# A PEER expert stage in two parts: U rows and dots first, then half of V's columns dense on TensorE and half gathered for VectorE

## What is computed

```python
q  = normalize((h @ wq).reshape(t, 8, 256))           # 8 heads
s1 = einsum('thd,hkd->thk', q[..., :128], subkeys[:, 0])   # 128 keys per half
s2 = einsum('thd,hkd->thk', q[..., 128:], subkeys[:, 1])
# top 16 of each half, top 16 of the 16 x 16 sums: 16 experts per token and head
idx  = i1 * 128 + i2                                   # of 16384 experts
gate = softmax(best_scores)
act  = gelu(einsum('td,tkd->tk', h, peer_u[idx]))      # 128 dots per token
out  = einsum('tk,tkd->td', act * gate, peer_v[idx])   # 128 rows added per token
y    = layer_norm(alpha * h_in + gt2 * out)
```

## Time and profile before

| | |
|---|---|
| median of three runs | 3455.93 us |
| span of the profiled execution | 3455.3 us (its time is not given apart from the span) |
| TensorE busy | 3200.0 us, 93% |
| VectorE busy | 1851.0 us, 54% |
| GpSimd busy | 918.8 us, 27% |
| ScalarE busy | 525.4 us, 15% |
| DMA moved | 989.40 MB, mean 286 GB/s; 420 to 428 GB/s from 2200 us to 3400 us |
| gathers | 536.90 MB, 37.0% of what 16 DMA engines could be busy |

### The profile page before, as it was taken

One profiled execution on the slowest core, in us unless ns is written; L12 is line 12 of the kernel. 1 busy time (PEld: TensorE's weight loads), 2 busy tenths in 40 slices (PEclk: granted clock), 3 DMA queues, 4 the chain that ended last, 5 costly groups with the idle time before them and its releaser, 6 DMA issues. The chain is left out here.

```text
span 3455.3 us, 30801 instructions
## 1 busy us (share of the span) xinstructions
PE 3200.0 (93%) x10108; PEld 1775.5 (51%) x10108; DVE 1851.0 (54%) x3355; ACT 525.4 (15%) x1056; POOL 918.8 (27%) x618
## 2 busy tenths in 40 slices
PE   6999999999999999999999999998987887878876
PEld 2467667575857576777644444443433333333332
DVE  6544444444444344666756434656566566565655
ACT  2312212121212121211000001111111111111110
POOL 0011112020202111100000002555555555555553
PEclk8999999999999999999999999999998898898988
DMA  9764554545463645545554597999999999999997
GB/s 359 288 227 179 188 185 175 200 169 209 149 231 132 231 163 205 205 170 192 200 180 170 171 342 296 398 427 423 427 421 423 423 426 424 426 427 427 426 427 311
DMA packets 152449, 989.40 MB, mean 286 GB/s; under 512 B 17771, under 2 KB 30764, under 8 KB 38572
## 3 DMA queue, kind: packets, MB, share of 16 engines
q0 software_dynamic: 73728, 536.90, 37.0%
q1 hardware_dynamic: 67104, 424.88, 33.9%
q10 hardware_dynamic: 11536, 26.55, 2.0%
HBM read 969.13 MB, written 19.14 MB: 286 GB/s over the span
## 5 line engine op out<-in xcount | busy, mean ns | idle before, releaser
L2535 PE MATMUL ps<-gates,diagonal 128*128 128x512 f32 x2048 | 992.2, 647 | 198.6 <-ACT diagonal L2163 198.6
L1075 PE MATMUL ps<-mT,ring 128*128 128x256 f32 (+1 forms) x4096 | 1168.9, 446 | 1.1 <-PEq L216 1.1
L1075 PEld LDWEIGHTS ps<-mT,ring 128*128 128x128 f32 x4096 | 775.0, 190 | 387.9 <-issue 318.2
L2352 DVE CUSTOM_DVE_ANT_0 u_rows<-u_rows,yhy 128x2048 f32<-128x2048 f32 x256 | 585.9, 2292 | 470.4 <-DMA u_rows<-in_peer_u_dram,expert_index 458.3
L2535 PEld LDWEIGHTS ps<-gates,diagonal 128*128 128x128 f32 x2048 | 420.5, 208 | 768.7 <-issue 637.9
L2096 POOL DMA_INDIRECT gates<-in_peer_v_dram,expert_index x256 | 418.9, 1636 | 502.8 <-PE ps L2535 417.3
L2096 POOL DMA_INDIRECT u_rows<-in_peer_u_dram,expert_index x256 | 273.6, 1069 | 135.8 <-issue 134.6
L707 POOL TENSOR_TENSOR dd<-mask_f,dt_g 128x1024 f32<-128x1024 f32 x16 | 30.3, 1896 | 933.0 <-DVE dt_g L977 932.4
L867 DVE SCALAR_TENSOR_TENSOR conv<-ps,tap_g,conv 128x510 f32<-128x510 f32 (+1 forms) x48 | 33.8, 704 | 338.7 <-ACT conv L728 338.7
L2157 ACT ACTIVATE gelu<-dot 128x4 f32<-128x4 f32 x64 | 13.1, 205 | 1059.2 <-DVE dot L2352 1059.2
L881 DVE SCALAR_TENSOR_TENSOR ada_sums<-ada_tiles,csil,ada_sums 128x1024 f32<-128x1024 f32 x120 | 153.9, 1283 | 4.0
(11 more groups left out here) (372 smaller groups left out, 2878.2 us busy)
## 6 DMA issues: line engine op xcount, KB each, us to landing
ring<-in_w_stream_dram SPq DMA_DIRECT2D x160, 1024.0 KB, 5.0
ada_tiles<-in_w_ada_dram SPq DMA_DIRECT2D x64, 1024.0 KB, 6.8
ring<-in_w_mix_dram SPq DMA_DIRECT2D x48, 1024.0 KB, 4.9
ring<-in_w_mod_dram SPq DMA_DIRECT2D x32, 1024.0 KB, 10.7
ring<-in_w_out_dram SPq DMA_DIRECT2D x32, 1024.0 KB, 5.4
rows<-cum_rows_scratch SPq DMA_DIRECT2D x16, 1536.0 KB, 13.1
ring<-in_w_q_dram SPq DMA_DIRECT2D x11, 1024.0 KB, 7.2
hf_scratch<-hf ACTq DMA_DIRECT2D x8, 768.0 KB, 6.4
```

Source lines behind the costliest of these rows:

```text
L1075: mm = nc.tensor.matmul(ps[:, k % 4, 0:n], m.ring[:, slot, kt * P:(kt + 1) * P], m.mT[:, kt, 0:n], start=(kt == 0), stop=(kt == KT - 1))
L2352: nc.vector.tensor_tensor_reduce(out=u_slot[n], in0=u_slot[n], in1=h2[:, t, :], scale=1.0, scalar=0.0, op0=ALU.mult, op1=ALU.add, accum_ou ...
L2535: return nc.tensor.matmul(ps[:, 4 * t + b, :], dia[:, (h % 2) * S + n, :], v_slot[n][:, b * CH:(b + 1) * CH], start=first and n == 0, stop ...
```

## The change

The expert stage gets two parts.

*Part one* gathers only U rows, through six slots (the four of `u_rows` and the two rows of `h_rows`, whose contents are first stored to a scratch tensor in memory). VectorE takes the dots of three rows in four (`dot_row`). Every fourth row (63 in all) goes to TensorE: 16 transposes of 128x128 blocks, which ScalarE copies out in quarters, then 16 products with the transposed tokens into one 128x128 bank, whose diagonal VectorE picks out (`take_diagonal`). The gelu and the coefficient come once per unit of 16 rows, not per batch.

*Between the parts* the 128 coefficients and key pairs of a token become a matrix. The gate and the two key indices are transposed, so that the pairs lie on partitions. For each token VectorE makes two 128x128 matrices (`one_hots`): first key equal to the column number times coefficient, and second key equal to the column number. TensorE multiplies them (`spread_tokens`), which gives for this token a 128x128 table of first key by second key, and ScalarE copies it to `W`. Tile 0's 128 tokens are spread between the batches of units 9 to 12, two groups of four tokens after each batch; tile 1's are spread after the last dot, with nothing of VectorE beside them.

*Part two* adds V. For columns 0 to 1023 TensorE reads V whole: 128 tiles of 128 experts x 1024 columns (0.5 MB, `v_dense`), each multiplied by `W` for both token tiles (`sum_tile`, two times two products of 512 columns). For columns 1024 to 2047 GpSimd gathers 256 half rows (0.5 MB, `v_rest`) into eight slots (four slots for the last 24), and VectorE adds each, scaled (`add_row`). The two tiles' rows are then finished together at the end. Query weights have four homes in place of five, and two of those are loaded only after VectorE's last modulation (`h2_p`).

The core of the diff:

```diff
 # GpSimd
-                with pool.Fori(0, UNITS) as u:
-                    for h in range(NB):
-                        pool.wait_ge(idx_v, NB * u + (h + 1))
-                        for slots, table, into, free in ((u_slot, d.peer_u, u_in, u_free), (v_slot, d.peer_v, v_in, v_free)):
...
+                for j in range(ROWS):
+                    if j % TOPK == 0:
+                        pool.wait_ge(idx_v, j // TOPK + 1)
+                    if j >= NU:
+                        row_taken(pool, j - NU)
...
+                    nc.gpsimd.indirect_dma_start(
+                        u_slot[j % NU], None, d.peer_u, bass.IndirectOffsetOnAxis(ap=eidx[:, j:j + 1], axis=0)).then_inc(u_in[j % NU], 16)
+                for k in range(ROWS):
+                    if k == 4:
+                        pool.wait_ge(dot_v, N_DVE)
+                        pool.wait_ge(turn_p, 4 * N_PE)
+                    if k >= 8:
+                        pool.wait_ge(acc_v, v_before(k)[0])
+                    pool.sem_inc(pool_step, 1)
+                    nc.gpsimd.indirect_dma_start(
+                        v_slot[v_at(k)], None, d.v_rest, bass.IndirectOffsetOnAxis(ap=eidx[:, v_pair(k):v_pair(k) + 1], axis=0)).then_inc(v_in[v_at(k)], 16)
 # SP
+                for i in range(NKEY):
+                    if i == 0:
+                        sp.wait_ge(dot_v, dve_rows(ROWS // 2 - 1))
+                    if i == 2:
+                        sp.wait_ge(dot_v, N_DVE)
+                    if i >= NVT:
+                        sp.wait_ge(vt_used, i - NVT + 1)
+                    sp.dma_start(v_tile[:, i % NVT, :], d.v_dense[i]).then_inc(vt_in[i % NVT], 16)
 # VectorE
+                def one_hots(t, n):
...
+                    for a in range(4):
+                        token = 4 * n + a
+                        s = 2 * (token % 8)
+                        nc.vector.tensor_scalar(one_hot[:, s, :], iota[:], by_pair[:, 1, token:token + 1], by_pair[:, 0, token:token + 1],
+                                                ALU.is_equal, ALU.mult)
+                        nc.vector.tensor_scalar(one_hot[:, s + 1, :], iota[:], by_pair[:, 2, token:token + 1], None,
+                                                ALU.is_equal).then_inc(hot_v, 1)
+                def add_row(k):
...
+                        nc.vector.scalar_tensor_tensor(acc[:, t, :], v_slot[v_at(k)], coefficient, acc[:, t, :],
+                                                       ALU.mult, ALU.add).then_inc(acc_v, 1)
+                for u in range(UNITS):
...
                     for h in range(NB):
+                        k = NB * u + h
                         for n in range(4):
+                            if not on_pe(4 * k + n):
+                                dot_row(4 * k + n)
+                        if k:
+                            take_diagonal(k - 1)
...
+                        for n in spread_at(u, h):
+                            one_hots(0, n)
+                coefficients(UNITS - 1)
+                for n in range(P // 4):
+                    one_hots(1, n)
+                for k in range(ROWS):
+                    add_row(k)
+                finish_late_columns()
+                finish_early_columns()
 # TensorE
+                def row_by_pe(k):
+                    j = 4 * k + 3
+                    pe.wait_ge(u_in[j % NU], 16 * (j // NU) + 16)
+                    turn_quarter(k, 0)
+                    turn_quarter(k, 1)
...
+                    dot_quarter(k, 0)
+                    turn_quarter(k, 2)
+                    dot_quarter(k, 1)
+                    turn_quarter(k, 3)
+                    dot_quarter(k, 2)
+                    dot_quarter(k, 3).then_inc(dot_p, 1)
+                def sum_tile(i):
+
+                    pe.wait_ge(vt_in[i % NVT], 16 * (i // NVT) + 16)
+                    for t in range(TT):
+                        for k in range(2):
+                            mm = nc.tensor.matmul(ps[:, 2 * t + k, :], W[t][i // HALF][:, i % HALF, :], v_tile[:, i % NVT, k * CH:(k + 1) * CH],
+                                                  start=(i == 0), stop=(i == NKEY - 1))
...
 # host layouts
-        "peer_u": p["peer_u"], "peer_v": p["peer_v"],
+        "peer_u": p["peer_u"],
+        "v_dense": p["peer_v"].reshape(NKEY, NKEY, D).transpose(1, 0, 2)[:, :, 0:D // 2],
+        "v_rest": p["peer_v"][:, D // 2:],
```

More of the change, by code:

```diff
@@ L1888, in _ @@
                 pe.wait_ge(tr_a, 8)
-def scale_shift(nc, v, c, rows, mean, rstd, g, b):
-    for x, mu in zip(rows, mean):
-        t = c.inc(nc.vector.scalar_tensor_tensor(x, x, mu, g, ALU.subtract, ALU.mult))
-    v.wait_ge(c.sem, t)
-    for x, r in zip(rows, rstd):
-        t = c.inc(nc.vector.scalar_tensor_tensor(x, x, r, b, ALU.mult, ALU.add))
-    v.wait_ge(c.sem, t)
 def block_ef(nc, m, d):
@@ L2460, in _ @@
[L2460 to L2468 removed]
+                        k = NB * u + h
+                        for n in range(4):
+                            if not on_pe(4 * k + n):
+                                dot_row(4 * k + n)
@@ new lines, in _ @@
+                        if k:
+                            take_diagonal(k - 1)
+                        if u < UNITS - 1:
+                            if h == 0:
+                                rank_halves(u + 1)
+                            elif h == 1:
+                                rank_pairs(u + 1)
+                            elif h == 2:
+                                weigh(u + 1)
+                        if h == 1:
+                            if u:
+                                coefficients(u - 1)
+                            if u in GROUPS_AT:
+                                normalise_queries(GROUPS_AT[u])
@@ L2500, in project_q @@
                     if 0 <= n < N_HOME:
-                        pe.wait_ge(home_in[n], 16 * len(homes[n]))
-                        per = 4 // len(homes[n])
-                        tile = [homes[n][kk // per][:, kk % per * CH:(kk % per + 1) * CH] for kk in range(4)]
+                        pe.wait_ge(home_in[n], 16)
+                        tile = [homes[n][:, kk * CH:(kk + 1) * CH] for kk in range(4)]
                     else:
@@ L2543, in batch @@
-                def batch(u, t, h, first=False, last=False):
-                    for n in range(S):
-                        await_row(u, h, n)
-                        for b in range(4):
-                            mm = row_product(u, t, h, n, b, first, last)
-                        mm.then_inc(v_free, 1)
-                def spread_row(n):
-                    if n == 0:
-                        pe.wait_ge(rows2_in, 48)
-                        pe.wait_ge(sc_a, len(PAIRS))
-                    else:
-                        pe.wait_ge(wide_a, n)
-                    for b in range(4):
-                        mm = nc.tensor.matmul(ps[:, 4 + b, :], m.ones[0:1, :], m.ring[0:1, n, b * CH:(b + 1) * CH], start=True, stop=True)
-                    mm.then_inc(wide_pe, 1)
@@ new lines, in spread_tokens @@
+                def spread_tokens(t, n):
+                    k = n + t * P // 4
+                    if n == 0:
+                        pe.wait_ge(pair_a, t + 1)
+                    if k >= 4:
+                        pe.wait_ge(w_a, 2 * (k - 3))
+                    for a in range(4):
+                        token = 4 * n + a
+                        s = 2 * (token % 8)
+                        pe.wait_ge(hot_v, P * t + token + 1)
+                        mm = nc.tensor.matmul(ps[:, 4 + k % 4, a * NKEY:(a + 1) * NKEY], one_hot[:, s, :], one_hot[:, s + 1, :], start=True, stop=True)
+                    mm.then_inc(spread_p, 1)
@@ L2590, in _ @@
                     project_q(*piece)
-                for u in range(SPLIT):
+                for u in range(UNITS):
                     for h in range(NB):
-                        batch(u, 0, h, first=(u == 0 and h == 0))
+                        k = NB * u + h
+                        if k < N_PE:
+                            row_by_pe(k)
                         done, new = turns_at(u, h)
```

498 lines of the change are left out of this document (281 added, 217 removed).

## The result

The changed kernel takes 3490.55 us (median; 3489.53 to 3493.18), the kernel before 3456.14 beside it: a ratio of 1.010, 95% interval 1.0086 to 1.0114. It is slower by 34 us; 3450 was predicted. The profiled execution took 3493.18 us with a span of 3491.5, against a predicted span of 3449: 42.5 us to find.

The account below looks back on a forecast made before the run. The DMA was taken as the bound: 63 MB less saves 147 us, eaten by the gap (45), one-hots (54), start and queries (29) and piece size (about 16), giving 3450 us; 8 in 10 between 3385 and 3535.

Parts of the forecast that it names:

- The failed step: Part one: DMA at 39.2 us and VectorE at 38.0 per unit of 16 U rows, imperfectly interleaved, take 40.0.
- the shallow queue: Rival for part one's twelve units: DMA at only 375 GB/s, +56 us, 3506 us in all; chance 0.12.
- SP's stores of h (2 MB) and two query homes: Start of part one: these transfers run beside the first dots; no time was put on them.
- The stall of 12 us on TensorE's first row: Unit 0: VectorE needs TensorE's first diagonal about 2169 and gets it at 2181, 12 us lost (0 to 25).
- "hidden" on ScalarE's copies: Part one: ScalarE's some 2.5 us of copies per batch cost no time of their own.
- 24 rows in four buffers: End of part two: the last 24 V rows through four slots were put at 5 us more.
- the gap: Between last dot and part two: 3.5 us plus tile 1's one-hots, 61.5 us; some 45 us of DMA lost.
- GpSimd not the bound in part two: Part two: 256 GpSimd issues take 317 us beside 479; the rival with GpSimd as bound, 3596 us, had chance 0.03.
- the sum: Whole kernel: the added terms give 3450 us; chance 0.42 for 3425 to 3480.
- The rival on TensorE: Part one: TensorE's row at 12 us against 10 in 48 batches sets the pace, +77, 3527 us; chance 0.14.
- The rule on GpSimd: GpSimd's issue waits for one two-input VectorE dot: 0.94 us beside idle or small work, 2.60 started in a dot.
- The rule on size: The skill wants 1 MiB a DMA; 384 are halved, but part two's 12 in flight were taken to cover it.

Follow-up runs that it names:

- e1: The changed kernel with ten U buffers in place of six for rows 16 to 143 (units 1 to 8); 3469.26 us.
- e6: The changed kernel with VectorE's dots made one-input sums of the U row, h2 left out; 3473.46 us (one run).
- e2: The changed kernel with all of a TensorE row's transposes ahead of its products; 3480.98 us.
- e14: The changed kernel with one-input sums for VectorE's dots and ten U buffers for rows 16 to 143; 3453.66 us (one run).
- e3: The changed kernel with TensorE's rows beginning only in unit 1, VectorE taking all 16 rows of unit 0; 3490.95 us.
- e15: e1 with only a quarter of the columns of the query weights loaded during the stage; 3456.90 us (one run).
- e10: The changed kernel with the edits of e1 and e2, and eight buffers for the last 16 V rows; 3451.29 us.
- e7: The changed kernel with VectorE's dots over 1024 of the 2048 columns; 3432.30 us (one run).

## Why the prediction was wrong

**The failed step.** It is the price of the hand-over in part one: "Two resources at 39.2 and 38.0 that hand each other six buffers (14.7 us of DMA) will not interleave perfectly; VectorE's longest block without a release is 6.4 us, under the buffers. I take 40.0." The work was right: VectorE's own unit is 37.2 us (e1), predicted 38.0. The hand-over was compared with one block of VectorE alone. A buffer's round has more in it: the issue held up by a dot (e6, 19.1 us of part one), TensorE's hold of the fourth row, whose last transposes stand behind half of the products (e2, 8.5 us), and then a place in the queue. These act on one quantity, and their gains don't add (e14); ten buffers cover most of it, 24.4 us. The rival that named it, the shallow queue, was the right mechanism, taken too strongly (+56 for twelve units): units 1, 3 and 5 to 8 were at 39.3 to 43.8, not at 44.7 throughout, and the whole came to 3490.6, not 3506.

**Bytes left out at the start.** "SP's stores of h (2 MB) and two query homes [...] run beside": they were costed at nothing, beside a DMA that is full from 2151 to 2190 us (418 GB/s). With the query weights of the ring they make the 10.3 MB, 24 us, of units 0 to 2. The stall of 12 us on TensorE's first row was predicted at the right place but is no term of its own there: taken away, it gave under 1 us in units 0 to 2 (e3). With 7.6 MB less in them, 11.9 us came back (e15), 7.2 of it in the two units whose DMA was full.

**A wait in neither the prediction nor an edit.** Before units 1, 3 and 5 VectorE waits for scores: 6.1, 6.7 and 5.4 us in the changed kernel. The last of them, from 2400 to 2560 us (view of waits, after: us in total, times, longest us):

```profile
DVE u_rows L2453 <- ACT scores L2213: 5.4, 1, 5.4
```

Before unit 1 TensorE is done with these scores at 2209.6 us, but ScalarE copies them at 2218.1, because its list has the four quarter copies of TensorE's next U row first. The prediction put "hidden" on ScalarE's copies, which looked at its busy time and not at its order. In e1 and e15 two of the waits are left, 6.7 to 6.8 us each, in units 0 and 2. No run takes them away, so what they cost beside the bytes stays open.

**The end of part two.** 5 us were put on 24 rows in four buffers; they cost some 12 more than with eight buffers for the last 16 (e10). It is the same mistake as in part one: the buffers' round wasn't worked out, here 7.4 us for four rows.

**What held.** VectorE's selection and dots, one-hots 0.45 a token, units 9 to 12 at 52.0 (52.5), the gap 61.9 (61.5), 128 tiles in 439.7 us (445), TensorE's row hidden, GpSimd not the bound in part two (299 us of 400), the tail. Pieces of 4 KB went at 420 GB/s; 1.27 us for 0.524 MB (412) was 2% too long. With the rounds covered (e10) the time was 3451.3, 1 us from the forecast: the sum was about that of a kernel with enough buffers. That it agrees so closely is luck. In e10 units 0 to 4 took 12 us more than the sum's, and units 5 to 8 (6), the first dot (4) and units 9 to 12 (2) gave it back.

**Two slips in the prediction's numbers.** The rival on TensorE sets 12 us against 10 in 48 batches, which is 48 x 2 = +96 us, not 48 x 1.6 = +77. And a profiled execution's time lies 1.7 us above its span here (3493.18 and 3491.5), not 0.6. Neither changes the outcome.

**The rule on GpSimd.** With a two-input dot an issue takes 1558 ns on average, with a one-input sum 949. The Trainium skill ("SBUF — State Buffer", Who interferes with whom) locks the shared ports for two-input VectorE work against a GpSimd operation that reads, and infers that the writing of descriptors goes on. The runs are in line with the first and not with the inference. e6 took away the write of the products together with the second input, so the runs don't say which of the two does it.

**The rule on size.** With some twelve half-megabyte transfers in flight the DMA moved 420 GB/s; with four rows, and the load of h beside them, 279. The Trainium skill ("DMA: Bandwidth & Descriptors", Bandwidth) asks for 1 MiB a DMA; by these rows depth decides more than size.

## What to carry to other kernels

Before a stage is costed by its busiest engine, add up one buffer's whole round (issue, landing, every engine that reads it, release) and divide it by the number of buffers; if that is above or near the resource's time per item (here 2.68 and 2.45 us), doubt that the stage reaches the resource's rate. More buffers can then be worth more than less work: in units 5 to 8 ten buffers took off 14 us (e1), half the dots' work 4 (e7). Count every byte in a stretch whose DMA is full, those of other queues too. Moving work into a gap helps only if the engine that sets the gap's length is not the one that does the work.
